# Feed-forward turns in quadrants exchanged through HBM, and a third seven-product group per quarter

## What is computed

```
x = x + jnp.einsum('bsd,de->bse', merged, w_out[l])
h2 = rms_norm(x, norm_ffn_g[l])
u = jnp.square(jax.nn.relu(jnp.einsum('bsd,df->bsf', h2, w_up[l])))
x = x + jnp.einsum('bsf,fd->bsd', u, w_down[l])
return rms_norm(x, norm_final_g)
```

## Time and profile before

| | us |
|---|---|
| median of 3 runs | 1476.15 |
| profiled execution | 1476.18 |
| its span, first to last instruction | 1474.4 |
| PE busy | 1465.7 |
| DVE busy | 1190.9 |
| ACT busy | 766.8 |

### The profile page before, as it was taken

One profiled execution on the slowest core, in us unless ns is written; L12 is line 12 of the kernel. 1 busy time (PEld: TensorE's weight loads), 2 busy tenths in 40 slices (PEclk: granted clock), 3 DMA queues, 4 the chain that ended last, 5 costly groups with the idle time before them and its releaser, 6 DMA issues.

```text
span 1474.4 us, 18772 instructions
## 1 busy us (share of the span) xinstructions
PE 1465.7 (99%) x6968; PEld 1279.8 (87%) x6968; DVE 1190.9 (81%) x1558; ACT 766.8 (52%) x986; POOL 15.0 (1%) x21
## 2 busy tenths in 40 slices
PE   9999999999999999999999999999999999999997
PEld 8888888888888888888888888888888888888886
DVE  7977887776577788777799988888897888889877
ACT  7656565444455555444445555555554555555553
POOL 0000000000000000000000000000000000000000
PEclk9999999999999999999999999999999999999999
DMA  9556544667655566556765665656666656655563
GB/s 333 191 169 211 184 154 164 229 203 241 213 180 184 186 199 206 194 200 200 248 233 181 202 219 201 218 185 207 217 204 202 208 199 226 214 199 193 198 209 114
DMA packets 149801, 299.33 MB, mean 203 GB/s; under 512 B 5232, under 2 KB 5360, under 8 KB 149488
## 3 DMA queue, kind: packets, MB, share of 16 engines
q1 hardware_dynamic: 149168, 297.51, 59.9%
q10 hardware_dynamic: 576, 1.06, 0.2%
HBM read 296.45 MB, written 2.10 MB: 202 GB/s over the span
## 4 chain that ended last, share of the span: by engine, by line
PE 98%; issue 1%; DVE 1%; POOLq 0%; POOL 0%; DVEq 0%; ACT 0%
PE acc L545 88%; PE acc L827 3%; PE banks L776 3%; PE acc L776 1%; PE banks L564 1%; PE banks L583 1%; PE banks L573 0%; PE banks L591 0%; DVE ta_lo L1775 0%; PE banks L680 0%; PE banks L696 0%; PE banks L695 0%; PE banks L693 0%; PE acc L603 0%; DVE final L1787 0%
## 5 line engine op out<-in xcount | busy, mean ns | idle before, releaser
L865 ACT ACTIVATE whi<-raw 128x1024 fp32r<-128x1024 f32 x542 | 569.2, 1056 | 577.3 <-PE acc L545 517.9
L1222 DVE TENSOR_TENSOR wlo<-raw,whi 128x1024 fp32r<-128x1024 f32 x542 | 655.1, 1223 | 213.1 <-ACT whi L865 208.5
L545 PE MATMUL acc<-whi,ta_hi 128*128 128x512 f32 x1308 | 497.4, 380 | 0.0
L545 PE MATMUL acc<-wlo,ta_hi 128*128 128x512 f32 x1308 | 495.7, 379 | 0.0
L545 PE MATMUL acc<-whi,ta_lo 128*128 128x512 f32 x1308 | 495.7, 379 | 0.0
L545 PEld LDWEIGHTS acc<-whi,ta_hi 128*128 128x128 f32 x1308 | 247.2, 189 | 36.7 <-issue 1.2
L545 PEld LDWEIGHTS acc<-whi,ta_lo 128*128 128x128 f32 x1308 | 247.2, 189 | 35.1
L545 PEld LDWEIGHTS acc<-wlo,ta_hi 128*128 128x128 f32 x1308 | 247.3, 189 | 34.5
L545 PE MATMUL acc<-whi,tb_hi 128*128 128x512 f32 x560 | 212.3, 379 | 0.0
L545 PE MATMUL acc<-wlo,tb_hi 128*128 128x512 f32 x560 | 212.2, 379 | 0.0
L545 PE MATMUL acc<-whi,tb_lo 128*128 128x512 f32 x560 | 212.2, 379 | 0.0
(11 more groups left out here) (208 smaller groups left out, 1049.2 us busy)
## 6 DMA issues: line engine op xcount, KB each, us to landing
raw<-in_w_in SPq DMA_DIRECT2D x64, 1024.0 KB, 5.2
raw<-in_w_up SPq DMA_DIRECT2D x64, 1024.0 KB, 5.3
raw<-in_w_down SPq DMA_DIRECT2D x57, 1024.0 KB, 5.0
raw<-in_w_gate SPq DMA_DIRECT2D x32, 1024.0 KB, 5.3
raw<-in_w_att SPq DMA_DIRECT2D x16, 1024.0 KB, 5.0
raw<-in_w_ret SPq DMA_DIRECT2D x16, 1024.0 KB, 5.0
raw<-in_w_out SPq DMA_DIRECT2D x16, 1024.0 KB, 5.0
raw<-in_w_down SPq DMA_DIRECT2D x14, 512.0 KB, 4.3
```

What stands on the lines that cost most here:

```text
L545: last = nc.tensor.matmul(paired(acc[B.parity][:, t, :]), a[:, k, tok], halves_in_turn(b), start=(k == 0 and n == 0), stop=(k == (B.ends + ...
L865: nc.scalar.activation(whi[:, B.ring_at(u), :], raw[:, B.raw_at(u), :], ACT.Copy).then_inc(hi_ready, 1)
L1222: V_.tensor_tensor(wlo[:, at, :], raw[:, B.raw_at(u), :], whi[:, at, :].bitcast(f32), ALU.subtract).then_inc(lo_ready, 1)
```

## The change

Each quarter's late groups are now given by a table: `LATE = {0:(0,1,3),2:(0,1,2)}`, which reads: up block 0 of the next quarter hosts the group of columns 0 and 1 over row group 3, up block 2 the group of columns 0 and 1 over row group 2. So D0 and D1 have 4 units instead of 6 in quarters 0 to 2. In the last quarter all 8 units of both are made, D0 and D1 first up to unit 5 and then their units 6 and 7 one after the other.

The turn takes 4 instructions over all 128 partitions (`turn_in_quads`), each turning its 32x32 quadrants in place, from a strided view of `buf[0]` into `buf[3]`. ScalarE's queue then stores `buf[3]` to a buffer in HBM (`park`, 512 KB) and loads it back with the rows in another order into `buf[1]` (`fetch`, 512 KB in runs of 256 elements), which does the exchange between the partitions. ScalarE waits for the store before it issues the fetch, and for the fetch before it makes `tb_hi`. For the second late group the tokens of row group 2 are fetched again and mixed again in up block 1.

T2 is now written to `buf[3]`, since `buf[1]` holds the fetched tokens, and waits for the park that reads `buf[3]`. The sums are made in another order. The gain of the last norm (`gfin`) is loaded at the end, because a second set of mixed tokens lies in its place.

The diff, cut:

```diff
+BOUNDARY = (2, 3, 3)
+LATE = {0:(0,1,3),2:(0,1,2)}
+EVERY = True
...
             def seven_products(G, J=None, K=None):
 
-                E, u = G.entries, UNITS - 2
+                E, u = G.entries, G.at
+                upper, lower = G.upper, G.lower
+                mixed_hi, mixed_lo = mixed_halves(G.c)
...
 (scalar, stage6)
+                for i in range(1 if first else 0, GROUPS):
+                    (E, tail), G = Q.up[i], Q.late[i]
+                    split(E, 0, 2)
+                    if i > 1:
+                        hi_from_exchanged(Q.turn(q, i - 1), i - 2)
+                    split(E, 2, 4)
...
+                        squared_relu(Q.up[i - 1][1])
...
+                    if G:
+                        split(E, 4, 5)
+                        if i:
+                            park(q * 4 + i, i - 1)
+                        split_for_seven(G, E, 5)
+                        split(tail, 6, 7)
...
+                    if i:
+                        fetch_next(Q, q, i, first)
+                    split(tail, 7, 8)
...
+            def park(n, g):
+
+                act.wait_ge(quads_turned, n)
+                act.dma_start(parking[g], in_quads.rearrange("p o n -> p (o n)")).then_inc(parked, 16)
+
+            def fetch(g, n):
+
+                act.dma_start(exchanged_at.rearrange("p i a n -> p i (a n)"),
+                              parking[g].rearrange("(i f) (o n) -> (f o) i n", f=SQ, o=QUADS)).then_inc(exchanged, 16)
...
+            def split_for_seven(G, B, begin, squares_of=None):
+
+                u = G.at
+                split(B, begin, u - 1)
                 if squares_of:
-                    residual_squares(squares_of, 1, down_sq)
-                sums_hi(G, 0)
-                sums_hi(G, 1)
-                split(B, 5, 6)
-                sums_hi(G, 2)
-                split(B, 6, 9)
+                    residual_squares(squares_of, 1, down_sq, buf[1])
+                sums_hi(G, 0, 1)
+                sums_hi(G, 1, 3)
+                sums_hi(G, 2, 3)
+                split(B, u - 1, u + 3)
                 act.wait_ge(sum_set, G.sums(SUMS + 1))
-                split(B, 9, 10)
+                split(B, u + 3, u + 4)
...
 (vector, stage6)
+                G = Q.boundary
+                split(Q.J, 0, 1)
+                split(Q.J, 1, 2)
+                mixed_tokens(Q.turn(q, 4), q * MIXES_OF_QUARTER)
+                if not last:
+                    lo_from_exchanged(q * 4 + 16, 3)
+                ready = min(Q.units[2] - 2, 3) if G else 3
+                split(Q.J, 2, ready)
+                mixed_lo_of(GROUPS - 1, q * MIXES_OF_QUARTER)
+                add_residual(Q.down_end[1], 1)
+                if G:
+                    split(Q.J, ready, G.at - 2)
+                    sums_for_seven(G, q * 4 + 4, G.mixed)
+                    fold_to_bank(G, Q.K, split_last if last else split)
...
+            def turn_in_quads(n):
+
+                dve.wait_ge(u_ready, n)
+                if later(n - 1):
+                    dve.wait_ge(parked, (n - 1) * 16)
+                strided = buf[0][:].rearrange("p t (m f o) -> p m t f o", o=QUADS, f=SQ)
+                for o in range(QUADS):
+                    piece = V_.transpose(in_quads[:, o, :].rearrange("p (m t n) -> p m t n", t=TILES, n=SQ), strided[:, :, :, :, o])
+                piece.then_inc(quads_turned, 1)
...
+            def sums_for_seven(G, parks, mixes):
...
+                V_.tensor_tensor(T1, left_up, right_up, ALU.add).then_inc(sum_set, 1)
+                dve.wait_ge(raw_full[E.slot(u + 2)], E.filled(u + 2))
+                dve.wait_ge(mixed_lo_ready, mixes)
+                V_.tensor_tensor(T3, right_up, right_low, ALU.add).then_inc(sum_set, 1)
+                split(E, u - 2, u - 1)
+                dve.wait_ge(sum_set, G.sums(2))
+                dve.wait_ge(parked, parks * 16)
+                V_.tensor_tensor(T2, T1, right_low, ALU.add).then_inc(sum_set, 1)
                 sums_lo(G, 0)
-                fourth_sum(G)
-                split(B, 5, 6)
+                split(E, u - 1, u)
+                dve.wait_ge(sum_set, G.sums(3))
+                V_.tensor_tensor(right_up, T2, left_low, ALU.add).then_inc(sum_set, 1)
                 sums_lo(G, 1)
-                split(B, 6, 8)
+                split(E, u, u + 2)
                 sums_lo(G, 2)
```

More of the change, by code:

```diff
@@ new lines, in stage6 @@
+            def stage6(q, first, last=False):
+                Q = Quarter(q, first, last)
+                for i in range(GROUPS):
+                    load_up(Q, q, i)
+                pairs = [n // 2 for n in Q.units]
+                if last:
+                    for j in range(2):
+                        load_rows(Q.down[j], w_down, j * COLS, q * D, range(3))
+                    for j in range(2):
+                        load_rows(Q.down_end[j], w_down, j * COLS, q * D, range(3, 4))
+                else:
+                    for j in range(2):
+                        load_rows(Q.down[j], w_down, j * COLS, q * D, range(pairs[j]))
+                load_rows(Q.J, w_down, 2 * COLS, q * D, range(pairs[2]))
+                if Q.boundary:
+                    load_left(Q.boundary, q * D)
+                    load_right(Q.boundary, q * D)
+                load_rows(Q.K, w_down, 3 * COLS, q * D, range(pairs[3]))
+                if last:
+                    if AGAIN:
+                        sp.wait_ge(folded, q * FOLDS_OF_QUARTER)
+                    sp.dma_start(gfin[:], g_fin.partition_broadcast(P)).then_inc(fin_full, 16)
@@ L761, in stage6 @@
-                gemm(B[5], tb_hi, tb_lo, 0, B[5].ends + 1)
-                gemm(B[6], tb_hi, tb_lo, 0, UNITS - 2)
-                if not last:
+                Q = Quarter(q, first, last)
+                for i in range(GROUPS):
+                    (E, tail), G = Q.up[i], Q.late[i]
+                    if first and i == 0:
+                        pe.wait_ge(h2T_ready, 3)
+                        gemm(E, ta_hi, ta_lo, 0, 6)
+                        pe.wait_ge(first_half, T_STAGE5 + 4)
+                        gemm(E, ta_hi, ta_lo, 6, 7)
+                        pe.wait_ge(h2T_ready, 4)
+                        gemm(E, ta_hi, ta_lo, 7, 8)
+                    else:
+                        gemm(E, ta_hi, ta_lo, 0, 6)
+                        if G:
+                            seven_products(G)
+                        gemm(tail, ta_hi, ta_lo, 6, 8)
@@ L832, in rest @@
             def rest(B):
-                for u in range(2, UNITS):
+                for u in range(B.ends + 1):
                     pe.wait_ge(lo_ready, B.low(u))
@@ new lines, in stage6 @@
+                split(Q.down[0], 0, 2)
+                hi_from_exchanged(Q.turn(q, 3), 2)
+                split(Q.down[0], 2, 4)
+                act.wait_ge(quads_turned, q * 4 + 3)
+                if Q.late[3]:
+                    act.wait_ge(sum_lo_ready, Q.late[3].halves(3))
+                squared_relu(Q.up[3][1])
+                if Q.units[0] > 4:
+                    split(Q.down[0], 4, 6)
+                split(Q.down[1], 0, 1)
+                park(q * 4 + 4, 3)
+                split(Q.down[1], 1, 3)
@@ new lines, in stage6 @@
+                fetch_next(Q, q, 4, first)
+                split(Q.down[1], 3, 4)
+                if last:
+                    hi_from_exchanged(Q.turn(q, 4), 3)
+                    split(Q.down[1], 4, 6)
+                    for j in range(2):
+                        split(Q.down_end[j], 6, 8)
+                elif Q.units[1] > 4:
+                    split(Q.down[1], 4, 6)
+                split(Q.J, 0, 2)
+                if not last:
+                    hi_from_exchanged(Q.turn(q, 4), 3)
```

420 lines of the change are left out of this document (241 added, 179 removed).

## The result

The changed kernel takes 1510.56 us (median of 4 runs, 1509.31 to 1511.26), the kernel before, on the same chip, 1476.3 us (4 runs, 1476.13 to 1476.61). The ratio is 1.0231, with a 95% interval of 1.0213 to 1.0249: slower by 34 us. The forecast was 1506.8, in a range of 1497 to 1524.

What follows compares the result with a forecast made beforehand. TensorE, 99% busy, was taken to bound the kernel, so time goes only by removing matmuls or making it wait. -3.9 + 2.6 + 11.0 + 7.3 + 13.6 = +30.6 on 1476.2 gives 1506.8 us, range 1497 to 1524.

Steps and rivals of the forecast that it cites:

- Saved: 18 matmuls, 3.9 us: Three more seven-product groups, each 42 matmuls instead of 48, take 18 matmuls off TensorE: 3.9 us less.
- The clock of a group: From host block start t and first sum T1 at S: fold starts at S+15.64, TensorE pauses (S - t) - 1.78 us.
- the rival without it (1490.2): In the groups, high parts do not hold back unit 5, so VectorE has no idle 2 us: 1490.2 us; chance 0.05.
- Boundary groups, 11.0 us for quarters 0 to 2, and 7.3 for the last: Mixing now stands later, delaying T1: pause 3.66 us three times, 11.0 us, and 7.3 us in the last quarter.
- Late group of the first up block, 2.6 us: List ahead of T1 unchanged, S = t+2.64: pause 0.86 us, three times, 2.6 us.
- Third up block, 13.6 us: New group behind the turn: T1 at t+5.36, T2 waits for a 4.3 us park, pause 4.5, three times: 13.6 us.
- the signs that I had named: TensorE waits at all ten groups, VectorE idle 2 us before unit 5's split, VectorE waiting for the park in third up blocks.
- The rival of four times the price (1523): A turn's 128-partition transpose costs four times as much, quadrants one after the other: +16 us, 1523; chance 0.04.
- Fetch from HBM: nothing: The load back from HBM, taken at 5.0 us, fits the time before its tokens are needed: cost nothing.
- The rival of a slow exchange (1521.5): Park takes 6.8 us and fetch 8.2, adding 14.7 us at third up blocks and boundary groups: 1521.5; chance 0.15.
- The clock: 0.02 for a fall in each group: Rival: pauses drop TensorE to 1.2 GHz for all 42 matmuls of each of ten groups, +90 us, 1597; chance 0.02.

Runs made afterwards that it cites:

- experiment 1: Changed kernel, with ScalarE's split of unit 5 put back ahead of the high parts of T2 and T3 in every group: 1493.1 us.
- experiment 2: Changed kernel without the third group of each quarter, the turns through HBM kept: 1498.18 us.
- experiment 3: Changed kernel with the turn's transposes reading elements in order instead of every fourth, columns coming out in wrong order: 1506.27 us.
- experiment 6: Changed kernel's work reordered on VectorE and ScalarE, plus transposes without stride and the fetch as four DMAs: 1475.96 us, ratio 0.9997.
- experiment 9: Changed kernel's work reordered on VectorE and ScalarE, plus T1 written several times over to make TensorE pause on purpose: 1526.94 us, one run.
- Experiment 8: Changed kernel with only the last quarter's mixing of the tokens moved a block earlier, behind the second down block's fourth split: 1508.22 us.
- experiment 5: Changed kernel's work reordered on VectorE and ScalarE, without the third group of each quarter: 1477.12 us, ratio 1.0005 to the kernel before.

## Why the prediction was right, step by step

**Saved: 18 matmuls, 3.9 us.** Right: 6950 for 6968.

**The clock of a group** (S of T1, 15.64 to the fold, lateness S - t - 1.78). Right nearly to the hundredth. At the boundary group of quarter 1, t is 1088.08:

```profile
1093.50 1.22 DVE L1890 TENSOR_TENSOR buf<-raw 128x1024 f32<-128x1024 f32 x1
...
1109.10 0.68 DVE L1966 TENSOR_TENSOR mix<-mix,banks 128x512 f32<-128x512 f32 x1
```

```profile
1109.83 0.48 PE L853 MATMUL banks<-sum_hi,mixed_hi 128*128 128x512 f32 x1 [1.15 <-DVE mix L1966]
```

S is t+5.42 (predicted t+5.44), the fold S+15.60 (15.64), the product S+16.33 (16.35), the lateness 3.61 (3.66). The idle time ahead of unit 5 is 1.88 us in all ten groups for the 2.0 predicted, and experiment 1 shows that it reached TensorE; the rival without it (1490.2) is what that experiment built, at 1493.1.

**Boundary groups, 11.0 us for quarters 0 to 2, and 7.3 for the last.** Measured 10.9 and 7.1. In the last quarter mixing, high part, squares and splits came in the predicted order, T1 at t+8.8 for t+9.0.

**Late group of the first up block, 2.6 us.** Undersized: 4.2. In quarter 1 it was 0.92 for 0.86. In quarters 2 and 3 T1 stood 0.6 and 1.1 us at a corner load. I had set the second fetch beside loads that leave 40% of the DMA time free and charged nothing; the mean share did not tell of the moment. But that the second fetch is the cause is not shown. Without it (experiment 2) quarter 2 is back at 0.85 us and quarter 3 keeps 1.48; with it, and shorter turns (experiment 3), they are at 0.71 and 0.97. What delays the loads stays open.

**Third up block, 13.6 us.** Undersized: 15.3, and near it for partly wrong reasons. Two terms were mis-sized and cancelled in part: T1 came 1.6 us later in each group than I had it, and 0.9 us that I had charged for the park did not come. I gave the four transposes 1.79 us by the row of 32 partitions; they took 3.11. The row's 256 elements a partition stood in order, in runs of 32, and these are a stride of four apart; experiment 3 measures the stride by itself. I said that T2 would wait for a park of 4.3 us; this one landed in 2.6, and T2 waited for nothing, so of the signs that I had named this one did not come. With the turn's later start and a hand-over of 0.25 us T1 is at t+6.99 and not t+5.36, and the lateness is 5.2 by the formula: the same formula, another entry. That the sum of the whole came within 4 us is in part this luck. "VectorE: DVE Perf Modes" of the Trainium skill (the three transpose paths), which I had set beside the lower price, fits the 413 ns of experiment 3 and says nothing of the stride.

The rival of four times the price (1523) falls: the price was 1.7 times the one I took (3.11 for 1.79 us).

**Fetch from HBM: nothing.** Right in the changed kernel: it took 5.8 us for the 5.0 assumed, and no wait of TensorE ends on it. The rival of a slow exchange (1521.5) falls with it. It is close, though: in four pieces, and in the last quarter, it was late in the profiled run of experiment 6, one of three long ones of eleven.

**The clock: 0.02 for a fall in each group.** One fall came, behind the pause of 2.5 us in quarter 2; three equal pauses had none. Columns as in experiment 9:

```profile
1197.00:1199.90 2.90, 0.38 (x3) 0.02 (x1) 1.30 (x2) 2.90 (x4) 0.00 (x0) 1.00 0.00 0
...
1201.00:1204.40 3.40, 3.40 (x10) 2.70 (x9) 3.40 (x4) 0.47 (x2) 0.00 (x0) 0.50 0.91 293
```

For 3.4 us the granted clock is 0.50, which is 1.2 GHz. And it cost nothing: from the matmul behind the pause to the third product 7.41 us went by in quarter 2 (1199.88 to 1207.29), and 7.41 in quarter 1 without a fall (1027.46 to 1034.87). The third product waits for VectorE's fold, which came no later; slow matmuls filled a wait that was there anyway. Experiment 8 had a fall behind the same pause in all three quarters, and the stretch was 7.41, 7.41 and 7.50 us, that of quarter 3 in the changed kernel, without a fall, 7.50. "TensorE: Matmul & The Clock Gate" of the Trainium skill (part 1) has an idle TensorE drop to half rate. The trace agrees behind one of its four pauses of 2.5 us, where the granted clock is 0.50, and not behind the other three. My rival took half rate for all 42 matmuls of a group; it held for some eight. (The expectation of experiment 9 calls this pause 2.68 us: it counts from start to start, less 0.216.)

**Not in the sum at all: the restart.** The second matmul behind a pause comes 0.29 to 0.32 us after the first (1109.83 and 1110.15) and not 0.216. Inside a group the lateness hides it; behind the third product it counts, 0.9 us over ten groups.

Mis-sized terms together: +1.6 (late), +1.7 (third up block), -0.3 (boundary), +0.9 (restarts), 3.9 us. The median lies 3.8 us over the forecast, the profiled execution (1511.26), from which these terms are read, 4.5.

## What to carry to other kernels

Where engines run their lists strictly in order, the place of an instruction can weigh more than the instruction: here one split behind the high parts of two sums cost 17.5 us, and the order of the same work 34 us, nearly nine times what the change could save. Work taken from an engine that nobody waits for was worth nothing (experiment 5), and work added to its list just ahead of a deadline cost in full; so count from the deadline back, not by the shares of busy time. When a row prices an operation that is new, its access pattern must match and not only its size.
